# One list of items for all engines, or one for each

## The reference, cut to what matters

```python
def decoder_layer(x, shift0, s0, kv_past, logf_past, lw):
    h = rms_norm(x, lw['attn_norm'])
    proj = h @ lw['w_in']
    ...
    y_rwkv, shift_new, s_new = rwkv7_group(p_rwkv, shift0, s0, ...)         # recurrence over the rows, 4 heads
    y_fox = fox_attention(q[:, :, fs], k_all[:, :, fs], v_all[:, :, fs], c_all, Q_BLOCK)    # 4 heads
    y_moba = moba_attention(q[:, :, ms], k_all[:, :, ms], v_all[:, :, ms], MOBA_Q_BLOCK)    # 4 heads
    y_sb = stick_breaking_attention(q[:, :, ss], k_all[:, :, ss], v_all[:, :, ss], Q_BLOCK) # 4 heads
    mix = jnp.concatenate([y_rwkv, y_att.astype(y_rwkv.dtype)], axis=-1)
    x = x + mix @ lw['w_out']
    h2 = rms_norm(x, lw['mlp_norm'])
    x = x + jnp.square(jax.nn.relu(h2 @ lw['w_mlp_up'])) @ lw['w_mlp_down']
    return x, kv_new, log_f.astype(x.dtype), s_new, shift_new
```

## Time and profile before

| | |
|---|---|
| time of one execution, median of 3 runs | 933.95 us (932.73 to 937.57) |
| span of the profiled execution, first to last instruction | 930.9 us, 21268 instructions |
| TensorE busy | 894.3 us, 96% |
| VectorE busy | 640.8 us, 69% |
| ScalarE busy | 452.0 us, 49% |
| TensorE's granted clock, mean | 0.994 of full speed |
| middle stage, 205 to 511 us: TensorE, VectorE, ScalarE busy | 285.8, 191.3, 151.0 us of 306 |

### The profile page before, as it was taken

One profiled execution on the slowest core, in us unless ns is written; L12 is line 12 of the kernel. 1 busy time (PEld: TensorE's weight loads), 2 busy tenths in 40 slices (PEclk: granted clock), 3 DMA queues, 4 the chain that ended last, 5 costly groups with the idle time before them and its releaser, 6 DMA issues.

```text
span 930.9 us, 21268 instructions
## 1 busy us (share of the span) xinstructions
PE 894.3 (96%) x8588; PEld 769.5 (83%) x8588; DVE 640.8 (69%) x1083; ACT 452.0 (49%) x771; POOL 63.0 (7%) x95
## 2 busy tenths in 40 slices
PE   6999999998999999979999999999999999999998
PEld 5999899998887667756655789978998899889986
DVE  5563377647756763665664662789988988988796
ACT  6422636313241466775562533453574456535751
POOL 0000112114500000000000000100110000000000
PEclk9999999999999999989999999999999999999999
DMA  8542787861200687648997704886889532443343
GB/s 270 181 137 69 160 203 198 241 133 62 83 6 3 216 283 241 221 141 282 305 397 259 246 20 137 206 271 183 244 211 258 191 91 93 179 136 92 132 143 144
DMA packets 73163, 164.47 MB, mean 177 GB/s; under 512 B 5918, under 2 KB 32126, under 8 KB 70890
## 3 DMA queue, kind: packets, MB, share of 16 engines
q1 hardware_dynamic: 59370, 124.26, 38.9%
q0 software_dynamic: 13696, 38.85, 17.9%
HBM read 156.55 MB, written 40.10 MB: 211 GB/s over the span
## 4 chain that ended last, share of the span: by engine, by line
PE 82%; DVE 11%; ACT 3%; DMA 2%; issue 2%; DVEq 0%; ACTq 0%; SPq 0%
PE PS L962 16%; PE PS L964 15%; PE PS L963 15%; PE PS L1154 7%; PE PS L1317 4%; PE PS L1389 2%; PE PS L1339 2%; PE PS L995 2%; PE PS L1277 2%; PE PS L1303 2%; PE PS L1425 2%; DVE WL L2924 1%; PE PS L1294 1%; PE PS L1629 1%; PE PS L1630 1%
## 5 line engine op out<-in xcount | busy, mean ns | idle before, releaser
L963 PE MATMUL PS<-WL,U 128*128 128x512 f32 x224 | 87.6, 391 | 0.0
L962 PE MATMUL PS<-WH,U 128*128 128x512 f32 x224 | 87.5, 390 | 0.0
L2037 ACT ACTIVATE WH<-Wraw 128x1024 fp32r<-128x1024 f32 x56 | 57.9, 1056 | 48.9 <-PE PS L964 19.9
L2924 DVE TENSOR_TENSOR WL<-Wraw,WH 128x1024 fp32r<-128x1024 f32 x56 | 66.9, 1219 | 7.9 <-ACT WH L2037 7.9
L1154 PE MATMUL PS<-AR 64*64 64x64 f32 x1912 | 61.6, 219 | 4.0 <-DVE AR L2508 1.4
L1154 PEld LDWEIGHTS PS<-AR 64*64 64x64 f32 x1912 | 58.5, 135 | 7.3 <-issue 4.2
L962 PE MATMUL PS<-WR,HR 128*128 128x384 f32 (+1 forms) x184 | 63.7, 346 | 0.8 <-issue 0.8
L962 PE MATMUL PS<-h2H,WH 128*128 128x288 f32 x208 | 61.4, 295 | 1.2 <-DVE rc L3046 1.2
L1317 PE MATMUL PS<-cst,AR 128*128 128x128 f32 x384 | 54.7, 286 | 7.6 <-ACT W L1915 7.6
L963 PE MATMUL PS<-h2L,WH 128*128 128x288 f32 x208 | 61.2, 294 | 0.0
L964 PE MATMUL PS<-h2H,WL 128*128 128x288 f32 x208 | 61.2, 294 | 0.0
(11 more groups left out here) (436 smaller groups left out, 2310.4 us busy)
## 6 DMA issues: line engine op xcount, KB each, us to landing
AR<-in_cache_kv SPq DMA_DIRECT2D x120, 384.0 KB, 4.8
tau<-in_w_mlp_down POOLq DMA_DIRECT2D x24, 1024.0 KB, 9.0
Wraw<-tau SPq DMA_DIRECT2D x16, 1024.0 KB, 4.8
Wraw<-in_w_mlp_up SPq DMA_DIRECT2D x14, 1024.0 KB, 5.6
Wraw<-in_w_mlp_down SPq DMA_DIRECT2D x12, 1024.0 KB, 5.1
W<-in_w_in SPq DMA_DIRECT2D x6, 1536.0 KB, 9.6
QK<-in_cache_kv SPq DMA_DIRECT2D x8, 384.0 KB, 5.4
AR<-in_x_prompt SPq DMA_DIRECT2D x4, 512.0 KB, 6.8
```

The lines of the kernel that those rows point to most:

```text
L962: mm(out, lH, rH, start=start, stop=False, skip_group_check=skip)
L963: mm(out, lH, rL, start=False, stop=False, skip_group_check=skip)
L2037: f(piece_half(WH, r, d, h), piece_half(Wraw, r, d, h), ACT.Copy).then_inc(w_hi, 1)
L2924: tt(piece_half(WL, r, d, h), piece_half(Wraw, r, d, h), piece_half(WH, r, d, h).bitcast(F32), SUB).then_inc(w_lo, 1)
```

## The change

`ORDER` is replaced by three lists, `PE_ITEMS`, `ACT_ITEMS` and `DVE_ITEMS`, one for each engine, and the steps that an item tied together have names of their own: `Kt` turns a key unit and `Ks` scores one, `Kc` copies half a unit (so `Kc10` and `Kc11` are unit 5), `Vt` and `Vv` turn probabilities and multiply by values, `Aw` weighs, `At` takes turned weights, `Af` softens, `An` scales, `Am` is `mid`, `Z...` are the steps on whole score rows, `Wo`, `Wl`, `Mh`, `Ml` split the output weights and the mix. Now `Ap i` and `Ay i` are of unit i. Pages are used in the same order as before. One wait is added on VectorE.

```diff
-        ORDER = []
-        for n in range(A_FROM):
-            ORDER += [("R", n)] + AFTER.get(n, [])
-        PLAN = """
...
+        PE_ITEMS = items("""
+            R0 R1 R2 R3 L0 L1 R4 R5 R6 R7 R8 R9 R10 R11 R12 R13 R14 R15 R16 R17 R18 As0 R19 R20 R21 R22 R23 R24 R25
...
+        ACT_ITEMS = items("""
...
+        DVE_ITEMS = items("""
+            L0 L1 R0 R1 R2 R3 R4 R5 R6 R7 R8 R9 R10 R11 R12 R13 L2 R14 R15 R16 R17 R18 R19 R20 R21 R22 R23 As0 R24 R25
...
-                elif what == "K":
+                elif what == "Kt":
...
                     turn_keys(i)
-                    if i % NU_K:
-                        score_keys(i - 1)
-                elif what == "N":
-                    score_keys(NU_K * (i + 1) - 1)
-                    turn_p(TURNED_EARLY[i] - 2)
+                elif what == "Ks":
+                    score_keys(i)
+                elif what == "Kn":
                     score_new(i)
...
-            def take_keys(u):
-                for m in (2 * u, 2 * u + 1):
-                    act.wait_ge(kt_ps, m + 1)
-                    if m >= 4:
-                        act.wait_ge(kt_used, m - 3)
-                    f(KTr[m % 4], PS[:, KEY_BANK[m] * 512:(KEY_BANK[m] + 1) * 512], ACT.Copy).then_inc(kt_ev, 1)
+            def take_keys(m):
+                act.wait_ge(kt_ps, m + 1)
+                if m >= 4:
+                    act.wait_ge(kt_used, m - 3)
+                f(KTr[m % 4], PS[:, KEY_BANK[m] * 512:(KEY_BANK[m] + 1) * 512], ACT.Copy).then_inc(kt_ev, 1)
...
-                elif what == "Ap":
-                    if i >= 2:
-                        take_p(i - 2)
-                    if is_sb(i) and i not in SOFTENED_AT.values():
-                        soften(i)
-                    if is_sb(i - 1):
-                        weigh(i - 1)
+                elif what == "Aw":
+                    weigh(i)
+                elif what == "At":
+                    take_p(i)
+                elif what == "Af":
+                    soften(i)
...
                 for a in range(2):
+                    dve.wait_ge(c_ps, AT["Y", a] + 1)
                     link(tt(S0[:, a], S0[:, a], pc[:, a, 8:16].unsqueeze(2).to_broadcast([128, DB, 64]), MUL))
```

More of the change, by code:

```diff
@@ L711, in build, with items @@
[L711 to L718, removed]
+        def items(text):
+            names = [(t.rstrip("0123456789"), t) for t in text.split()]
+            return [(kind, int(t[len(kind):])) for kind, t in names]
@@ L719, in build @@
+        """)
+        PAGES = [(PE_ITEMS.index(("Kt", 3 * s)), "K", s) for s in range(NB_G * NPG)]
+        PAGES += [(PE_ITEMS.index(("Vv", g * NJ + p)), "V", g * NPG + p) for g in range(NB_G) for p in range(NPG)]
         PAGES = [(kind, s) for at, kind, s in sorted(PAGES)]
@@ L722, in build @@
         RING = [x for x in PAGES if x not in SPARE]
-        KEYS_AHEAD = sum(ORDER.index(("K", u)) < ORDER.index(("V", 0)) for u in range(NB_G * NU_K))
+        KEYS_AHEAD = sum(PE_ITEMS.index(("Kt", u)) < PE_ITEMS.index(("Vt", 0)) for u in range(NB_G * NU_K))
         KEY_BANK = [(0, 1, 3)[m % 3] if m < 2 * KEYS_AHEAD else m % 2 for m in range(2 * NB_G * NU_K)]
@@ L1448, in _ @@
             rwkv = rwkv_products()
-            for what, i in ORDER:
+            for what, i in PE_ITEMS:
                 if what == "R":
@@ L1456, in _ @@
                 elif what == "As":
-                    if i < NU:
-                        scores(i)
+                    scores(i)
                 elif what == "Ap":
-                    if i >= 2 and i not in TURNED_EARLY:
-                        turn_p(i - 2)
+                    turn_p(i)
                 elif what == "Ay":
-                    if i >= 2:
-                        times_v(i - 2)
-                elif what == "K":
+                    times_v(i)
+                elif what == "Kt":
                     if i == 0:
@@ L1472, in _ @@
                     turn_keys(i)
-                    if i % NU_K:
-                        score_keys(i - 1)
-                elif what == "N":
-                    score_keys(NU_K * (i + 1) - 1)
-                    turn_p(TURNED_EARLY[i] - 2)
-                    score_new(i)
[L1479 to L1489, removed]
+                elif what == "Ks":
+                    score_keys(i)
+                elif what == "Kn":
+                    score_new(i)
+                elif what == "Vt":
+                    turn_probs(*divmod(i, NJ))
+                elif what == "Vv":
+                    times_values(*divmod(i, NJ))
+                elif what == "Ob":
+                    pe.wait_ge(pv_ev, NU)
+                    sample_output(0, range(2))
+                    output(1, 1)
+                elif what == "Vr":
                     turn_result(i)
@@ L2786, in _ @@
             rwkv, norm = rwkv_steps(), rwkv_end()
-            LOW_AT = (None, None, (0,), (1, 2), (3, 4))
-            for what, i in ORDER:
+            for what, i in DVE_ITEMS:
                 if what == "R":
@@ L2792, in _ @@
                     log_sums(i)
-                elif what == "G" and i:
+                elif what == "G":
                     next(norm)
+                elif what == "Am":
+                    mid(i)
                 elif what == "As":
-                    if is_sb(i - 1):
-                        mid(i - 1)
-                    if i < NU:
-                        front(i)
-                elif what == "Ap":
-                    if 1 <= i <= NU and not is_sb(i - 1):
-                        scale_p(i - 1)
+                    front(i)
+                elif what == "An":
+                    scale_p(i)
                 elif what == "Ay":
-                    if i >= 2:
-                        take_y(i - 2)
+                    take_y(i)
                 elif what == "B":
```

118 lines of the change are left out of this document (60 added, 58 removed).

## The result

The changed kernel takes 907.55 us (median of 4 runs, 905.78 to 911.04), the kernel before on the same chip 933.34 (4 runs, 932.51 to 937.57): a ratio of 0.972, 95% interval 0.969 to 0.975, 25.8 us faster. The direction and the stretch were right; the size was not.

The account below looks back on a forecast made before the run. TensorE, busy 96%, was taken as the bound. Tiling 5.5, key copies 10.2, clock 3.0 and forget sums 1.0 make 19.7 us; less 3.5 given back, 16.2 off 933.95 gives 917.8 us, range 908 to 930.

Parts of the forecast that it names:

- Which stretch, and what bounds it: TensorE bounds the kernel; time can come from its waits and slow matmuls between 205 and 511 us.
- Changes of tiling: TensorE's tiling changes 182 times instead of 220; 38 fewer at 0.145 us each gain 5.5 us.
- Key copies freed: Key copies no longer behind attention units on ScalarE; waits at L1317, L1325 and L1367 go, gaining 10.2 us.
- Clock: TensorE's stretches at 1.2 GHz after long waits go with those waits, gaining 3.0 us.
- the other waits: TensorE's remaining idle time in 205 to 511 us, 9 us in pieces of 1.5 and less, stays.
- the forget sums: Forget-gate sums stand first on VectorE and L1 before R4 on TensorE; the wait of L1261 goes, gaining 1.0 us.
- nearly all of it: Rival, chance 0.17: the lists also take away most of the other 9 us; gain 23, 911 us.
- Given back: New losses on ScalarE, at the first output weights and at the end, 3.5 us, taken off the 19.7 gained.
- (a): ScalarE, 82% busy in 352 to 425 us, brings new short waits; 2.0 us given back.
- (b): First piece of output weights, issued by GpSimd after the new tokens' scores, comes late by some 0.5 us.
- (c): At the end, the second piece of output weights, issued by SyncE, comes late; 1.0 us with the hand-overs.
- named as a sign of being wrong: The forecast is wrong if a wait on AR<-in_cache_kv, a page load, appears; no size given.

Follow-up runs that it names:

- old_copies: Kernel before, only ScalarE's list changed: key copies moved ahead of softening and weighing of attention units in three places; 932.93 us, ratio 1.0007.
- old_one_place: Kernel before, only ScalarE's order changed at the place of the longest wait (key copies 64 to 69); 933.96 us, ratio 0.9991.
- old_helpers: Kernel before, between key units 30 and 42 ScalarE's order new, VectorE's new in part, TensorE's old; 933.38 us, ratio 0.9991.
- retied: Changed kernel, with softening of unit 17 and weighing of unit 16 back ahead of key copies 64 to 67 on ScalarE; 914.26 us, ratio 0.9787.
- head_new: Kernel before, with only the items up to the first key unit in the changed kernel's order; 931.62 us, ratio 0.9991.
- tail_new: Kernel before up to the first key unit, everything from there on in the changed kernel's order; 916.07 us, ratio 0.9826.

## Why the prediction was off, step by step

- **Which stretch, and what bounds it**: right. The stage gives 26.0, the rest of the program 0.
- **Changes of tiling, 5.5 us**: right. 38 x 0.134 = 5.1. The Trainium skill, page "TensorE: Matmul & The Clock Gate", section "Step-by-step: what each phase is for", tells of about 128 cycles until the last column has left the array; taken as the drain at a change that is an estimate of 0.053 us, and the measured price here is two and a half times that.
- **Key copies freed, 10.2 us**: the waits on L1317, L1325 and L1367 went entirely, and the arithmetic for the longest (0.9 us to spare, found 0.5) held, since it took TensorE's new order as its measure. The name was wrong: freed copies by themselves are worth nothing (old_copies, old_one_place, old_helpers), and TensorE's order by itself costs 13.5 us in one place.
- **Clock, 3.0 us**: right in kind, 1.00 throughout, and retied shows the loss come back with a wait. The size was too small by about 1.6. The forecast took the whole wait of 4.2 us out of the 10.2 us at the low level, but most of the wait passed before the clock fell. Windows of the kernel before:

```profile
404.93:406.06 1.13, 0.00 (x0) 0.00 (x0) 0.00 (x0) 1.13 (x3) 0.00 (x0) 0.50 0.73 293
406.06:411.76 5.70, 5.70 (x32) 3.44 (x33) 3.37 (x8) 4.74 (x14) 0.00 (x0) 0.50 0.02 4
```

  With 3.41 us more at the low level from 340.08 on, 9.1 us were worked at half speed: 4.6 us lost, not 3.0.
- **The step that failed: "I leave the other waits, 20.2 - 11.2 = 9 us in pieces of 1.5 and less, as they are."** It kept them without a reason. Idle time fell to 6.8, of which 2.7 are new or given back (below), so 4.1 of the 9 are left and 4.9 went. Of the kernel before (205 to 530 us) these waits went or fell:

```profile
PE PS L1154 <- DVE AR L2508: 1.4, 2, 1.0
PE PS L1294 <- DVE HM L2676: 1.4, 3, 0.5
PE PS L1303 <- ACT W L1872: 0.9, 2, 0.5
PE PS L1277 <- DVE HM L2676: 0.8, 2, 0.4
PE PS L1206 <- DVE AR L2559: 0.7, 1, 0.7
```

  3.0 of the 4.9 lie in the stretch of the recurrence, to which the forecast gave 1.0 us for the forget sums and little else: up to the first turned key the waits sum to 7.3 us before and 3.3 after. head_new, whose list is new only up to there, has lost the same ones (1.7 us besides waits for issue, as in the changed kernel; 5.9 before), and tail_new still has them. The rival *nearly all of it*, at 0.17, had said that most of the 9 go, and was nearest.
- **Given back, 3.5 us**: (a) ScalarE's short waits were 0.2, not 2.0; (b) the first piece of output weights 1.5, not 0.5; (c) the end 0, not 1.0; and a wait of 1.0 for a value page, named as a sign of being wrong, came and had no price. Sum 2.7, 0.8 less than forecast; that the total is so near is luck, for 2.8 too much in (a) and (c) stands against 2.0 too little in the two waits for DMAs. ScalarE was as full as feared in (a), busy 50.5 of 58 us (352 to 410), 87% and not 82, and still let TensorE wait only 0.2. The wait for the weights, in the chain of waits after:

```profile
440.73 10.63 DMA rc<-in_w_out
...
451.61 3.67 PE PS L1445 x8
```

  The transfer took 10.63 us, not the 9.7 of the earlier trace rows: the 0.9 are all but the whole error.
- **What was not in the sum**: the time from start to start without idle fell by 12.6, forecast 8.5 (5.5 and 3.0). The other 4.1 can be located by a count over all matmul records of the stage, each measured from its start to the next one's and set against the mean of its pair of lines at full clock in both traces. Fewer changes of tiling are 5.1, as the runs with extra matmuls say. The low clock is 4.9 (4.6 by the windows above). 1.6 are edges of waits: the last record before a wait runs to its end instead of being overlapped by the next, about 0.1 us for each of 25 waits before and 8 after, which the table of waits does not list. 0.9 are stalls at hand-overs from one line to another, too short for that table. Together they are 12.5 of the 12.6.

In numbers, for the stage: forecast 16.2; other waits +4.9, less given back +0.8, clock, edges of waits and short stalls together +4.1 make 26.0. For the time of a run: 9.8 of the error of 10.2 are these, the later start took 1.2 back, and the forecast let stand that the median lies 3.05 us above the profiled span, where it is 1.45 after, 1.6 less.

Still open is how much of the 9 us that head and page part give only together is real in the medians: some 4 to 5 are lost at the seams, the rest is seen in single traces of a recurrence that scatters by 3 us.

## What to carry to other kernels

When three in-order engines run from one plan, a wait removed at one engine can move to the next item that TensorE asks for, and the idle sum stays: in the one place measured, with TensorE's old order, 7.3, 6.6, 6.8 and 7.2 us for four orders of the helpers. There the sum fell only when TensorE's list gave the helpers time just where their chain is long, and the helpers' lists let everything past that does not belong to the chain. So judge such a plan by the sum of waits over the place, not by the one wait that was aimed at, and try the lists of all engines together: the helpers' part by itself measured as worthless, TensorE's as harmful. And look through the small waits as well before leaving them as they are: here they were the largest error.

## What the hardware showed that was not expected

A change of tiling, between transposes of 128*128 and products of 128*32, costs 0.134 us as the mean of both directions, with nothing else in the way. The granted clock fell within a wait and not behind it: 1.1 us before the end of the wait of 4.2 us in the kernel before, 2.5 us before the end of the one of 5.3 us in retied; 5.7 and 4.3 us of work behind them ran at 1.2 GHz. In the recurrence TensorE has waits with no releaser ("issue") whose length changes from one execution to the next of the same order: at about its 800th record 0.39 us before and 1.29 in old_helpers; at about the 680th 1.82 in old_copies, old_one_place and tail_new and none before. Together with the landing of a transfer (in_rc, 209.6 us before, 210.6 in tail_new) they move the recurrence's last product by 3 us at the same list (102.4 us from its start before, 105.4 in tail_new). That is more than most single edits here are worth, so that only medians of several runs can judge these.
